# Three seams of a two-layer kernel: the first item behind each with 128 tokens stationary, its weights split ahead of the seam

## The reference

```python
def modulate(h, shift, scale):
    return h * (1 + scale[:, None, :]) + shift[:, None, :]

# first_block
h = modulate(rms_norm(x, g_pre_mix), shift1, scale1)
mix = ...                                   # attention and mLSTM branches, @ w_out
x = x + gate1 * rms_norm(mix, g_post_mix)
h = modulate(rms_norm(x, g_pre_ffn), shift2, scale2)      # seam 1
f = (silu(h @ w_ffn_gate) * (h @ w_ffn_up)) @ w_ffn_down
x = x + gate2 * rms_norm(f, g_post_ffn)

# second_block
x = layer_norm(x, emb_ln_g, emb_ln_b)
h = x * (1.0 + sc1) + sh1                                  # seam 2
p = h @ w_in                                 # pu, pv (512 each), r, k, v, lora
y_a = gmlp_spatial_gating(p[..., :512], p[..., 512:1024], ...)  # uses layer_norm(gelu(pv))
y_b = rwkv7_time_mix(p[..., 1024:], ...)
mix = concatenate([y_a, y_b]) @ w_out
x = layer_norm(ALPHA * x + gt1 * mix, ln1_g, ln1_b)
h = x * (1.0 + sc2) + sh2                                  # seam 3
gu = h @ w_ffn_in
f = (silu(gu[..., :2816]) * gu[..., 2816:]) @ w_ffn_out
x = layer_norm(ALPHA * x + gt2 * f, ln2_g, ln2_b)
```

## Time and profile before

| what | value |
|---|---|
| median of 3 runs | 805.28 us |
| lowest and highest | 802.53 and 805.87 us |
| the profiled execution's own time | 803.44 us |
| its span | 801.6 us |
| mean granted clock of TensorE | 0.993 |
| busy: TensorE, weight loads | 766.2 us, 699.0 us |
| busy: DVE, ACT, POOL | 628.1, 394.6, 40.7 us |
| instructions | 15845, of them 6610 matmuls |
| DMA | 173.69 MB, mean 217 GB/s |

### The profile page before, as it was taken

One profiled execution on the slowest core, in us unless ns is written; L12 is line 12 of the kernel. 1 busy time (PEld: TensorE's weight loads), 2 busy tenths in 40 slices (PEclk: granted clock), 3 DMA queues, 4 the chain that ended last, 5 costly groups with the idle time before them and its releaser, 6 DMA issues.

```text
span 801.6 us, 15845 instructions
## 1 busy us (share of the span) xinstructions
PE 766.2 (96%) x6610; PEld 699.0 (87%) x6610; DVE 628.1 (78%) x811; ACT 394.6 (49%) x558; POOL 40.7 (5%) x61
## 2 busy tenths in 40 slices
PE   4999999889999999999999999999999999999996
PEld 3798888889789999998878987889768999999874
DVE  5869979988988887877868899886697688555447
ACT  3368834765464445443445885532225455445340
POOL 0123000000000000000002000050010000000000
PEclk9999989999999999999999999999999999999998
DMA  9897856764659999998983644500265589666621
GB/s 344 310 326 222 286 196 197 243 224 135 220 172 310 321 309 308 345 319 298 366 267 98 233 115 135 175 4 23 90 233 158 160 274 331 197 196 189 202 84 52
DMA packets 98070, 173.69 MB, mean 217 GB/s; under 512 B 7767, under 2 KB 55230, under 8 KB 97998
## 3 DMA queue, kind: packets, MB, share of 16 engines
q1 hardware_dynamic: 95678, 166.62, 62.7%
q0 software_dynamic: 1872, 5.86, 2.3%
q10 hardware_dynamic: 448, 0.19, 0.1%
HBM read 171.60 MB, written 1.05 MB: 215 GB/s over the span
## 4 chain that ended last, share of the span: by engine, by line
PE 73%; DVE 16%; ACT 5%; DMA 3%; issue 3%; DVEq 0%; SPq 0%; ACTq 0%
PE bank L2129 14%; PE bank L2130 13%; PE bank L2131 13%; PE bank L2402 5%; PE bank L2403 5%; PE bank L2404 5%; PE bank L2104 3%; PE bank L2105 2%; PE bank L2106 2%; DMA raw<-in_w_ada 2%; DVE wlo L473 2%; DVE acc L500 2%; PE bank L2564 1%; ACT whi L694 1%; DVE xn L1566 1%
## 5 line engine op out<-in xcount | busy, mean ns | idle before, releaser
L473 DVE TENSOR_TENSOR wlo<-raw,whi 128x1024 fp32r<-128x1024 f32 (+1 forms) x212 | 254.7, 1214 | 82.9 <-ACT whi L694 79.3
L694 ACT ACTIVATE whi<-raw 128x1024 fp32r<-128x1024 f32 (+1 forms) x212 | 220.0, 1051 | 193.1 <-PE bank L2131 78.4
L2129 PE MATMUL bank<-hh,whi 128*128 128x256 f32 x1016 | 284.2, 280 | 3.0 <-DVE hl L1222 2.9
L2131 PE MATMUL bank<-hh,wlo 128*128 128x256 f32 x1016 | 281.8, 277 | 0.0
L2130 PE MATMUL bank<-hl,whi 128*128 128x256 f32 x1016 | 281.8, 277 | 0.0
L2129 PEld LDWEIGHTS bank<-hh,whi 128*128 128x128 f32 x1016 | 190.7, 188 | 6.2 <-issue 5.6
L2131 PEld LDWEIGHTS bank<-hh,wlo 128*128 128x128 f32 x1016 | 191.8, 189 | 0.0
L2130 PEld LDWEIGHTS bank<-hl,whi 128*128 128x128 f32 x1016 | 190.8, 188 | 0.5 <-issue 0.5
L2402 PE MATMUL bank<-whi,ffh 128*128 128x512 f32 x168 | 65.7, 391 | 0.9 <-DVE wlo L473 0.9
L2403 PE MATMUL bank<-wlo,ffh 128*128 128x512 f32 x168 | 65.4, 390 | 0.0
L2404 PE MATMUL bank<-whi,ffl 128*128 128x512 f32 x168 | 65.4, 389 | 0.0
(11 more groups left out here) (453 smaller groups left out, 1073.9 us busy)
## 6 DMA issues: line engine op xcount, KB each, us to landing
raw<-in_w_ada SPq DMA_DIRECT2D x96, 512.0 KB, 5.3
raw<-in_w_in SPq DMA_DIRECT2D x54, 512.0 KB, 4.6
raw<-in_w_ffn_in SPq DMA_DIRECT2D x88, 256.0 KB, 4.0
raw<-in_w_ffn_gate SPq DMA_DIRECT2D x44, 256.0 KB, 4.6
raw<-in_w_ffn_up SPq DMA_DIRECT2D x44, 256.0 KB, 5.6
raw<-in_w_ffn_down SPq DMA_DIRECT2D x22, 512.0 KB, 5.5
raw<-in_w_ffn_out SPq DMA_DIRECT2D x22, 512.0 KB, 4.3
raw<-in_w_out SPq DMA_DIRECT2D x16, 512.0 KB, 4.0
```

Source lines behind the costliest of these rows:

```text
L473: eng.tensor_tensor(lo[:, 0:nk * width], raw[:, b % RAW, 0:nk * width], hi[:, 0:nk * width].bitcast(fp), ALU.subtract)\
L694: act.activation(weight_place(g)[0][:, 0:nk * width], raw[:, b % RAW, 0:nk * width], ACT.Copy)\
L2129: mm(o, wh[:, k, c], xh[:, kk_, :], start=first, stop=False)
L2131: last = mm(o, wl[:, k, c], xh[:, kk_, :], start=False, stop=end)
```

## The change

1. **Item form.** ff0, pv and gf0 become the first items behind seams 1, 2 and 3; pv moves in the stream from behind v to ahead of lora. All three are computed by a new `seam_out`: 128 tokens stationary, 512 weight columns moving, first rows first. The order on TensorE is: transposes of the first rows (`turn_rows(u, 0)`), high part of the first half of the features (hh by high and low weights, 16 matmuls of 512 columns in two blocks), low part of it (hl by high weights), high part of the second half, transposes of the second rows, low part of the second half, then the same for the second rows without the transposes.
2. **Halves.** Scaling, rounding and subtraction are done by row halves and feature halves: `scale_even` and `round_h` on ACT, `scale_odd` on DVE, and the low part of the first rows by POOL (`first_low`), that of the second rows by DVE (`second_rows`).
3. **Weights ahead of the seam.** The split weights of ff0, pv and gf0 get places of their own in the arena (`seam_at`); their high and low parts are made ahead of the seam. The low parts of ff0's blocks 0, 2 and 3 and of all four blocks of gf0 are made by POOL (`ON_POOL`), behind gate_bias(5) and gate_bias(11). pv's blocks stand among the last blocks of dA (`AMONG_DOWN`) on SP, ACT and DVE, and are made by DVE.
4. **ff0 and gf0 come out with tokens on the partitions**, so the product of silu and up is turned back by eight transposes (`turn_products`) inside the next item; ACT and DVE split it from PSUM there.
5. **Moved.** Piece 3 goes from seam 1 into `turn_ym` (inside ba1), with its collection on DVE. Pieces 8 and 9 stay in seam 2, collected on DVE before the second rows. The eight transposes of the first rows of seam 3 stand inside the last block of wo3b's second rows, and `ln_rows(1, 0)` stands ahead of the wait for wo2b. gelu(pv), its variance and the Sqrt go ahead of lora's copies; `normalise_v(0)` stands after r's preparation and `normalise_v(1)` after the first two blocks of pu. pu is prepared where pv was. The fillers of the seams go, but for six behind the first transposes of seam 1.

The diff, cut to its core:

```diff
-    middle = ["lora", "k", "r", "v", "pv", "pu", "wo2a", "wo3a", "c21", "wo2b", "wo3b"]
+    middle = ["pv", "lora", "k", "r", "v", "pu", "wo2a", "wo3a", "c21", "wo2b", "wo3b"]
+AMONG_DOWN = (("dA9", 0), ("pv", 0), ("pv", 1), ("dA9", 1), ("pv", 2), ("dA10", 0), ("pv", 3), ("dA10", 1))
+SEAM = {1: "ff0", 2: "pv", 3: "gf0"}
+ON_POOL = {"ff0": (0, 2, 3), "gf0": (0, 1, 2, 3)}
...
+        seam_at = {"ff0": (6144, 8192, 13312, 15360), "pv": (0, 2048, 5632, 7680), "gf0": (6144, 8192, 13312, 15360)}
...
+            def first_low(u):
+                for half in range(2):
+                    pool.wait_ge(sem("hh_ready"), 4 * u + half + 1)
+                    x = (slice(None), slice(4 * half, 4 * half + 4), slice(0, P))
+                    pool.tensor_tensor(hl[x], hx[x], hh[x].bitcast(fp), ALU.subtract).then_inc(sem("h_ready"), 1)
...
             gate_bias(5)
+            prepare_on(pool, "pool", "ff0")
+            first_low(1)
             pool.wait_ge(sem("h_ready"), 8)
...
             gate_bias(10)
+            first_low(2)
...
             gate_bias(11)
+            prepare_on(pool, "pool", "gf0")
+            first_low(3)
...
+            gelu("pv", gv)
+            act.wait_ge(sem("pads"), 11)
             split("k")
+            act.wait_ge(sem("var_ready"), 2)
+            act.activation(st[:, 132:134], st[:, 132:134], ACT.Sqrt).then_inc(sem("std_ready"), 1)
             b0, b1 = item("lora")
...
+            def second_rows(u):
+                for half in range(2):
+                    scale_odd(u, 1, half)
+                for half in range(2):
+                    dve.wait_ge(sem("h_ready"), 4 * u + 2 + half)
+                    dve.wait_ge(sem("hh_ready"), 4 * u + 3 + half)
+                    x = (slice(None), slice(4 * half, 4 * half + 4), slice(P, 2 * P))
+                    TT(hl[x], hx[x], hh[x].bitcast(fp), ALU.subtract).then_inc(sem("h_ready"), 1)
...
             for m in range(MT):
+                if m:
+                    scale_odd(1, 0, 0)
                 dve.wait_ge(sem("post_squares"), 3 + m)
                 weighed(m, 1, w1[m])
-                post_rstd(0, m)
                 if m:
                     dve.nop().then_inc(sem(f"pair{place['wo1'][0] % 2}_free"), 1)
+                    scale_odd(1, 0, 1)
+                post_rstd(0, m)
                 add_rows(m)
                 dve.nop().then_inc(sem("x_added"), 1)
-                if m:
-                    collect_part(3)
-                    gains(1, v1T[:, v1["g_pre_ffn"][0]:v1["g_pre_ffn"][1]])
-                else:
-                    prepare("ff0", slice(0, 1))
+                if m == 0:
+                    prepare("ff0")
...
+            scale_odd(2, 0, 0)
             post_rstd(1, 1)
             add_rows(1)
+            scale_odd(2, 0, 1)
             for h in range(2):
                 ln_part(1, h)
             ln_var(1)
+            dve.wait_ge(sem("piece_done"), 10)
             collect_part(8)
             collect_part(9)
+            ln_rows(0, 1)
+            second_rows(2)
+            prepare("lora")
...
             prepare("r", slice(1, 3))
+            normalise_v(0)
...
-            prepare("pv", slice(0, 2))
+            prepare("pu", slice(0, 2))
+            normalise_v(1)
             shift_item(8, 12, "v", 4)
...
             ln_var(0)
+            ln_rows(1, 0)
             item("wo2b")
             residual(1, 0, w0[1])
...
+            for half in range(2):
+                scale_odd(3, 0, half)
             item("wo3b")
...
+            def seam_out(u):
+                name = SEAM[u]
+                banks = start_item(name)
+                g0 = place[name][1]
+                for m in range(MT):
...
+                    t = slice(m * P, (m + 1) * P)
+                    for half in range(2):
+                        n = 4 * u + 2 * m + half + 1
+                        two = (g0 + 2 * half, g0 + 2 * half + 1)
+                        pe.wait_ge(sem("hh_ready"), n)
+                        for g in two:
+                            i, nk, wh, wl = weights(g)
+                            for k in range(nk):
+                                x = hh[:, nk * i + k, t]
+                                mm(banks[m][:, :], x, wh[:, k, :], start=g == g0 and k == 0, stop=False)
+                                mm(banks[m][:, :], x, wl[:, k, :], start=False, stop=False)
+                        if m == 0 and half:
+                            turn_rows(u, 1)
+                        pe.wait_ge(sem("h_ready"), n)
+                        for g in two:
...
+                                last = mm(banks[m][:, :], hl[:, nk * i + k, t], wh[:, k, :], ...)
...
+                    if m == 0:
+                        part(3)
...
-            part(3)
-            turn_h(1, lambda m: xn[:, m * D:(m + 1) * D], "xn_ready", 2, 13, 2 * (place["wo1"][0] % 2))
+            turn_rows(1, 0)
+            run_on(6, start_bank("ff0"))
...
+                        if m and x and g > g0:
+                            turn_rows(3, 0)
```

353 lines of the change are left out of this document (219 added, 134 removed).

## The result

The changed kernel takes 831.21 us (median of four runs, 831.14 to 831.6), the kernel before 804.2 (four runs, 802.53 to 805.87): 1.034 times as long, 95% interval 1.031 to 1.037. It is slower, as forecast, but by 27 us where the forecast had 7, and outside its range. The profiled execution took 831.6 us, span 829.8.

A forecast was written before the change was run, and what follows sets the result against it. TensorE, busy 766 of 801.6 us, was taken as the bound; -1.45 + 2.3 - 4.3 + 5.35 + 2.7 + 2.3 = +6.9 on the profiled execution's 803.44 gave 810.3 us, range 800 to 817.

The forecast's parts named there:

- I take one such fall in seam 3, +2.3: Behind a 6 us hole in seam 3 TensorE's clock falls to half speed once: +2.3 us, bounds 0 and 4.6.
- stood in gaps and cost nothing: The filler matmuls that the change removes were taken to be free, so removing them was given no price.
- Whether DVE's tensor_scalar of 0.75 us (L1602) is held too no row shows; I let it run: Beside POOL's subtractions only two-input DVE instructions are held; the tensor_scalar runs on; the opposite would add 3.1 us.
- Rival C: DVE's tensor_scalars are held by POOL too, 2.2 us in seam 1, 0.85 in seam 3: 813.4 us, or 815.7; chance 0.20.
- Seam 1: ff0 ends at 247.25, 2.9 us earlier; with piece 3 and the product's transposes in ff1, -1.45 us.
- the wait in seam 3: In gf0, TensorE waits 6 us for h_ready, as first_low is queued behind POOL's subtractions; seam 3's term is +2.7 us.
- turn_products adds eight transposes to ff1 and to gf1, 0.9 us each, nothing hides them; its ACT and DVE steps replace those of the old item one for one: In ff1 and gf1, turning the product back costs TensorE 0.9 us each; ACT and DVE get no extra steps.
- no load is late by it: SP now waits on POOL for raw slots of ff0's and gf0's blocks, which come free no later than before.
- Tail of dA: At dA's end DVE has eight subtractions in place of four, the last ending 418.95 against 416.70: +2.3 us, loads hidden.
- Seam 2: From dA's end E, pv ends E+16.35 and lora E+24.55; with pv's old 10.9 us gone, -4.3 us.
- The middle: Without pv's cover DVE is late: TensorE waits 2.5 us in r and 2.85 in pu, +5.35 us, bounds 0 and 5.65.
- Piece 3: Moved from the first seam into turn_ym, it takes 1.6 to 1.7 us, of which 1.06 is idle time: 0.55 us added.

## Why the prediction was wrong

The sign was right and so was most of the list of places; the size was not. The forecast was +6.9 on a profiled execution, measured are +28.2. Where the 21.3 us between them lie:

- **Clock: the step "I take one such fall in seam 3, +2.3" (with two falls as its upper bound) failed.** There are nine stretches at the lower clock with some 20 us of busy time lost, one with 3.4 before: up to some +16.5 in place of +2.3, by this count two thirds of what was missing. The forecast wrote of the fillers that go that they "stood in gaps and cost nothing", and put nothing for taking them out. The run of the kernel before without the 100 of its seams shows these to be worth 8 to 9 us, and the changed kernel with fillers in its waits won 7.8, some 7 of it where they stand. The falls at 102, 129, 371 and 447 stand behind no long wait; what sets them off stays open.
- **Port: the step "Whether DVE's tensor_scalar of 0.75 us (L1602) is held too no row shows; I let it run" failed.** Rival C, which had it held, was right on this (its sign was 2 us or more in seam 1; it was 2.64) and too cheap. Seam 1 was to last 17.5 us from wo1's end and lasted 20.3: the tensor_scalar took 1.9 longer, and a fall of the clock cost up to 1.7. Rival C put 0.85 on seam 3; measured were 8.4, for there it waited for all four of POOL's subtractions. It did so in all five profiled kernels that have them in this place (9.07 to 9.23 us) and took 0.81 in the other nine. The forecast had looked for the wait in seam 3 at the low parts of the first rows, 6 us; it stood one step earlier and was 8.85. That the seam's total came out near the forecast all the same is luck. The Trainium skill, "SBUF — State Buffer", section Who interferes with whom, says that tensor_scalar can enter a mode in which it takes the shared ports, and that whoever comes second blocks for the whole instruction. The trace agrees on the first; on the second it goes further, a whole run of instructions (9.16 us beside 9.25).
- **ff1: the step "turn_products adds eight transposes to ff1 and to gf1, 0.9 us each, nothing hides them; its ACT and DVE steps replace those of the old item one for one" failed.** There are four transposes, not eight, so that price was too high. The steps of ACT and DVE are the same, but now someone on TensorE waits for them in the next item, and they stand behind a weight block on ACT. 7.0 us in place of 0.9, 2.3 of it the clock. The forecast asked who waits for a wait only where the change added a semaphore to an old order, and did not follow ACT's queue through the first item behind the seam, nor SP's: "no load is late by it" was wrong, the loads stood still for 9 us. The order of ACT's queue decided; with the Silu put first, the late block cost nothing.
- **Tail of dA: a term mis-sized,** +2.3 forecast, +5.7 measured: waits of 1.62 and 1.82, 3.4 in all, and 2.7 of clock behind them. The forecast counted DVE's subtractions and held the loads to be hidden; the run with pv's blocks spread took 2.4 us back without a subtraction less.
- **Seam 2:** to k E+24.55 forecast, E+26.6 measured; the fall at 447 costs 1.7 of the 2.1. Right but for the clock.
- **The middle: right in mechanism.** A wait of 2.5 ahead of the head sums was forecast, 2.32 measured; one of 2.85 in pu, 1.55 measured. The clock added 1.5. Not forecast: POOL's two masks and DVE now meet the other way round, and a second DVE instruction waits for POOL (timelines of DVE, the changed kernel and then the kernel before):

```profile
541.92 3.46 DVE L1989 TENSOR_TENSOR arena<-arena,cst 128x1024 f32<-128x1024 f32 x1
545.53 3.17 DVE L1999 TENSOR_TENSOR arena<-arena,cst 128x1024 f32<-128x1024 f32 x1
```

```profile
521.41 1.23 DVE L1856 TENSOR_TENSOR arena<-arena,cst 128x1024 f32<-128x1024 f32 x1
```

In the kernel before only the one of the earlier trace rows did, its neighbour took 1.23. That is 2.2 us on DVE, and 2.0 in TensorE's waits (1.45 and 1.12 for 0.56). It is no chance of one execution: the first of the two took 3.46 or 3.47 in all ten profiled kernels that have pv moved, and 1.22 or 1.23 in the four that have it in its old place. Why the order of the two engines turns round was not tested.
- **Piece 3: right.** From the first transpose of turn_ym to ba1's next matmul TensorE takes 2.53 us in place of 2.07, 0.46 against 0.55 forecast. wo1's end came 1.3 later, with up to 1.7 more of clock ahead of it.

By the count: clock 14.2 more than forecast, ff1 4.4 (its wait), the port in seam 1 1.9, the masks 2.0, the tail 1.1 (its waits of 3.4 for 2.3), and 1.3 less in pu: 22.3, against 21.3 to be explained. The terms are not independent, since part of the clock's cost lies ahead of waits that hide it, so that the sum comes near is no proof of each of them. Seam 3's larger wait hardly enters, because the forecast had booked 6 us at its neighbour.

The signs by which the forecast said it could be told: POOL's start right behind the broadcasts, the wait ahead of the head sums, that in pu's third block and that at dA's last block all came; "ff0 ending 17.5 us after wo1" did not (20.3), nor did the wait in gf0 stand where it was said.

## What to carry to other kernels

Filler matmuls are part of the schedule: before a change takes them out, or opens a hole behind them, price what TensorE does in the next stretch at half speed, for every hole and not for the longest. Do not let a run of GpSimd instructions without a pause overlap a tensor_scalar from SBUF to SBUF on the critical path (0.81 us became 9.16 here), and break up runs of two-input DVE instructions when GpSimd's result is awaited; the order within a seam decides which of the two is starved. And when work is moved ahead of a seam, ask what kept the loads going there before: blocks consumed inside the seam emptied the slots, and the engine that is last in a seam (here DVE) is not made shorter by giving TensorE its work earlier.
